# Gated delta rule inside a 256-token block: query scale as a logarithm in the gates, output norm from one product with ones, the value part of u from four whole products

## The chip, the cores and the metric

The kernel runs on one core of a Trainium2 chip. The metric is device time in microseconds (us) of one execution; lower is better. PE is TensorE (matmuls), PEld its weight loads, DVE is VectorE, ACT is ScalarE, POOL is GpSimd, SP issues DMAs.

## The reference, cut to what matters

The program computes a whole block: a mixer with a gated delta rule and cross attention, a second mixer, and a mixture of experts. Only the delta rule is touched. It has 24 value heads of width 128 over 256 tokens, in chunks of 64, with 12 query/key heads, each shared by two value heads:

```python
q = jnp.repeat(l2_norm(q), rep, axis=2) * DN_HEAD_DIM ** -0.5
k = jnp.repeat(l2_norm(k), rep, axis=2)
gc = jnp.cumsum(g, axis=-1)
...
sol = lax.linalg.triangular_solve(m, rhs, left_side=True, lower=True, unit_diagonal=True)
u0, w = sol[..., :dv], sol[..., dv:]
qk = jnp.einsum("bhncd,bhnjd->bhncj", q, k) * decay
q_dec = q * jnp.exp(gc)[..., None]
def step(state, inp):
    u = u0_c - jnp.einsum("bhcd,bhde->bhce", w_c, state)
    o = jnp.einsum("bhcd,bhde->bhce", qd_c, state) + jnp.einsum("bhcj,bhje->bhce", qk_c, u)
    state = cd_c[..., None, None] * state + jnp.einsum("bhcd,bhce->bhde", kd_c, u)
    return state, o
...
o = rms_norm(o.astype(p.dtype), out_g)
```

## The kernel before

All work is float32. Weights stream from memory in 466 units. Each unit has two halves. For each half ACT copies the weights to a rounded part (WH, line 2369, a CAST) and DVE makes the remainder (WL, line 1661), both three halves ahead of the matmuls that use them. PE then runs 24 matmuls of a half, in four pieces of six instructions. I call such a piece a fill. After a unit of the mixer's projections, ACT and DVE take the result out: for a value column by a convolution (ACT tap, three DVE operations, ACT Silu), for a gate column z by one ACT Silu.

The order on every engine is written by one class, `Plan`, that all engines replay. Each engine then executes its own list in order and waits on semaphores. In `mix`, two groups of two value heads are live at a time (a group is one query/key head; 12 groups), and after every step of a group one fill is put in. `group` (line 301) gives the steps of a group g:

- `dn_in`: PE makes X (inverse factors), A (k times q) and transposes of k and v into PSUM banks bA, bB, bC. It waits for `yn` of group g-2, which had the same buffers.
- `dn_decay`: DVE forms dT, the gap of summed gates (d1); ACT takes Exp of it (eT) and of qd (eB).
- `dn_uc`, `dn_low`, `dn_w`: PE products UC and W; ACT takes them out (un, nw); DVE scales k and v (k, v0), and multiplies A into dT (mark `qk`, line 1895), on POOL qd is multiplied by the query.
- four chunk steps: `dn_u(n)` on PE gives u in bank bA, ACT takes it out with the key's scale RNK (ut0 to ut3), `dn_o(n)` on PE gives the output o and the state's increment s, DVE adds it to the state (S0, S1, S2).
- `dn_y`: ACT takes the output out, POOL squares it. `dn_yss`: PE sums the squares over the head's width by four products into one column each; DVE adds the epsilon (scaled by the query's norm, EPSQ); ACT Sqrt; DVE reciprocal of 128x4. `dn_ybc`: PE spreads the 128x4 result over the partitions by four products. `dn_yn`: DVE multiplies it into the output.

Group g+2 starts when g ends, and the two live groups run about half a group apart. In steady state, while an odd group p ends (`dn_yss`, `dn_ybc`, `dn_yn`), the next even group e goes through `dn_decay`, `dn_uc`, `dn_low`, `dn_w` to its `dn_u(0)`. A pair below is the time from one even group's `dn_u(0)` to the next one's. Earlier, `rn_root` computes the scales of the 12 keys and queries, `iv_turn` transposes the summed gates, and `invert` inverts the chunk matrices on DVE.

Of the kernel before, what the change touches and what calls it, by code (L numbers as in the profile page):

```python
# [38 lines left out]
VEC = {}  # L39
# [126 lines left out]
class Plan:  # L166
# [485 lines left out]
def build(nc, D, out, scratch):  # L652
    ctx = ExitStack()
    with ctx:
# [30 lines left out]
        def f(kb, n):  # L685
            return view(kb, n, F)
# [110 lines left out]

        def dn_u(g):
            return dn(g, "US")[:, 0:256]

        def dn_s(g):
# [3 lines left out]
        IV_KK, IV_E, IV_TMP, IV_STG = f(94, 4096), f(110, 3072), f(78, 512), f(88, 1536)  # L805
        IV_GC, IV_BE, IV_GB = f(77, 64)[0:NI, :], f(77.25, 64)[0:NI, :], f(76, 256)[0:48, :]
        IV_U, IV_T = f(94, 2048), f(102, 2048)
        BEN = f(77.5, 48)
        EPSQ = vec[:, VEC["alog"][0]:VEC["alog"][0] + 24]
        iv_kk = IV_KK[0:NI, :].rearrange("p (r c) -> p r c", c=64)  # L810
# [228 lines left out]
        def tensor_program(e):  # L1039
# [340 lines left out]

            def dn_u_(g, n):
                bA = dn_bank(g)[0]
                t, b = n // 2, 64 * (n % 2)
                if n:
                    need_a(g, f"ut{n - 1}")
                    need_v(g, f"S{n - 1}")
                else:
                    need_a(g, "nw")
                    need_v(g, "qk")
                for h in range(2):  # L1390
                    i = 2 * h + t
                    o = PS[b:b + 64, bA, h * 128:h * 128 + 128]
                    m = mm(o, blk(dn(g, "U"), i)[:, b:b + 64], blk(dn(g, "bv"), i), True, n == 0)
                    if n:
                        m = mm(o, blk(dn(g, "X"), i)[:, b:b + 64], blk(dn_s(g), h), False, True)
                mark(g, f"u{n}", m)

            def dn_o(g, n):

                _, bB, bC = dn_bank(g)  # L1400
                t, b = n // 2, 64 * (n % 2)
                need_a(g, f"ut{n}")
                need_g(g, "qd")
# [5 lines left out]
                def from_within(h, start, stop):  # L1409
                    o = PS[:, bC, h * 256 + t * 128:h * 256 + t * 128 + 128]  # L1410
                    return mm(o, dn_u(g)[:, h * 128:h * 128 + 128], blk(dn(g, "dT"), 2 * h + t), start, stop)

# [9 lines left out]
                if n < 3:  # L1422
                    for h in range(2):
                        i = 2 * h + t
                        m = mm(blk(PS[:, bB, :], h), blk(dn(g, "kdc"), i)[b:b + 64, :],
                               dn_u(g)[b:b + 64, h * 128:h * 128 + 128], True, True)
                    mark(g, f"s{n}", m)

            def dn_yss(g):
                bA = dn_bank(g)[0]  # L1430
                need_g(g, "ysq")
                for i in range(4):
                    m = add_up(bA, i, blk(dn(g, "kb"), i))
                mark(g, "yss", m)

            def dn_ybc(g):
                bB = dn_bank(g)[1]
                need_v(g, "yrc")
                for i in range(4):
                    m = spread(blk(PS[:, bB, :], i), dn_s(g)[:, i:i + 1], C("ident"))  # L1440
                mark(g, "ybc", m)

# [189 lines left out]
            def end():  # L1632
                for d in range(4):
# [6 lines left out]
                  "iv_product": iv_product, "dn_in": dn_in, "dn_uc": dn_uc, "dn_w": dn_w, "dn_u": dn_u_, "dn_o": dn_o,  # L1640
                  "dn_yss": dn_yss, "dn_ybc": dn_ybc, "bias": bias, "ki_out": ki_out, "index": index,
                  "v2_turn": v2_turn, "aw": aw, "at": at_, "av": av, "pm": pm, "mean": mean, "stat": stat_,
# [4 lines left out]
        def vector_program(e):  # L1647
# [243 lines left out]
            def dn_low(g):  # L1891
# [20 lines left out]

            def dn_yss(g):
                rr = dn_s(g)[:, 0:4]
                eps = EPSQ[:, 2 * g:2 * g + 2].unsqueeze(1).broadcast_to([128, 2, 2])
                need_p(g, "yss")
                mark(g, "ysc", stt(rr.rearrange("p (h t) -> p h t", h=2),
                                   PS[:, dn_bank(g)[0], 0:4].rearrange("p (h t) -> p h t", h=2), 1.0 / 128, eps, ALU.mult,
                                   ALU.add))
                need_a(g, "yrt")  # L1920
                mark(g, "yrc", recip(rr, rr))

            def dn_yn(g):
                y = tile(VT, 2 * g, 2)
                need_p(g, "ybc")
                mark(g, "yn", stt(y, y, vc("outg"), PS[:, dn_bank(g)[1], :], ALU.mult, ALU.mult))

# [374 lines left out]
            def end():  # L2302
# [23 lines left out]
                for t in range(2):  # L2326
# [11 lines left out]
                  "rn_root": rn_root, "iv_product": iv_product, "iv_decay": iv_decay, "iv_scale": iv_scale,  # L2338
                  "iv_step": iv_step, "iv_out": iv_out, "dn_decay": dn_decay, "dn_uc": dn_uc, "dn_low": dn_low, "dn_o": dn_o, "dn_yss": dn_yss, "dn_yn": dn_yn, "y_split": y_split, "x1_out": x1_out,
                  "bias": bias, "ki_out": ki_out, "index": index, "topk": topk, "v2_turn": v2_turn, "aw": aw, "an": an,  # L2340
# [8 lines left out]
        def scalar_program(e):  # L2349
# [176 lines left out]
            def dn_u_(g, n):  # L2526
                t, b = n // 2, 64 * (n % 2)
                need_p(g, f"u{n}")
                mark(g, f"ut{n}", act(dn_u(g)[b:b + 64, :], PS[b:b + 64, dn_bank(g)[0], 0:256], ACT.Copy,
                                      scale=RNK[b:b + 64, 2 * g + t:2 * g + t + 1]))  # L2530

# [210 lines left out]
        def gpsimd_program(e):  # L2742
# [305 lines left out]
```

## Time and profile before

| | us |
|---|---|
| median of 3 runs | 2946.03 (2945.89 to 2946.81) |
| profiled execution, its own time | 2935.69 |
| its span from first to last instruction | 2933.9 |
| PE busy in the span | 2807.8 (96%) |
| DVE, ACT, POOL busy | 1926.1, 1371.3, 380.8 |

The profiled execution took 10.3 us less than the median of the timed runs. A busy engine is one with an instruction in it; instructions on PE overlap, so that a row's busy time divided by its count is closer to what one costs than its mean length. A plain float32 matmul stands as two instructions in the trace (x8 is four products).

### The profile page before, as it was taken

How to read it: one execution, taken by the hardware profiler on the slowest of the kernel's cores; microseconds unless marked ns; L12 is line 12 of the kernel's file. 1: busy time of each engine (PE TensorE's matmuls, PEld its weight loads, DVE VectorE, ACT ScalarE, POOL GpSimd, SP SyncE). 2: the span in 40 equal slices, each digit the busy share in tenths (PEclk: the TensorE clock that was granted, in tenths of full speed). 3: DMA queues.
4: the chain of work that ended last, by engine and by line, in shares of the span. 5: the costliest groups of instructions: out<-in, count | busy, mean ns of one | idle time of the engine just before them, and what ended most of it. 6: DMA issues, size and time to landing. Idle time of an engine off the chain costs nothing.

```text
span 2933.9 us, 46174 instructions
## 1 busy us (share of the span) xinstructions
PE 2807.8 (96%) x19298; PEld 2646.5 (90%) x19298; DVE 1926.1 (66%) x2862; ACT 1371.3 (47%) x2241; POOL 380.8 (13%) x360
## 2 busy tenths in 40 slices
PE   6999989999999999999989999998999999999996
PEld 6999989889989998999979999997888899987785
DVE  5546668544445445665458666776888888878886
ACT  5446544455545334444354114443555555555554
POOL 0000020211111000005000002221212111112210
PEclk9999999999999999999989999999999999999998
DMA  5444555523324554544425469998999988899993
GB/s 190 173 158 144 172 143 173 167 88 115 100 99 170 187 184 149 187 144 166 158 105 183 163 210 364 367 362 325 363 378 370 352 324 323 321 352 350 342 348 143
DMA packets 109679, 668.46 MB, mean 228 GB/s; under 512 B 25776, under 2 KB 26312, under 8 KB 31552
## 3 DMA queue, kind: packets, MB, share of 16 engines
q1 hardware_dynamic: 83808, 496.08, 46.6%
q0 software_dynamic: 24512, 164.97, 15.3%
q10 hardware_dynamic: 1152, 4.47, 0.4%
q8 instruction: 153, 2.51, 0.3%
q14 instruction: 54, 0.44, 0.0%
HBM read 651.54 MB, written 13.30 MB: 227 GB/s over the span
## 4 chain that ended last, share of the span: by engine, by line
PE 75%; DVE 12%; DMA 6%; ACT 5%; issue 2%; SPq 0%; POOL 0%; DVEq 0%; ACTq 0%
PE PS L1043 75%; DVE WL L1661 4%; DVE m L1652 3%; DMA raw<-in_pv 2%; ACT WH L2369 2%; DMA m<-in_pv,keep 2%; ACT m L2354 1%; DMA m<-s_kk 1%; DVE m L1861 1%; PE PS L1046 1%; DMA raw<-in_w_kv 1%; ACT m L2355 1%; DVE m L1858 0%; ACT L2354 0%; DMA raw<-in_pu 0%
## 5 line engine op out<-in xcount | busy, mean ns | idle before, releaser
L1661 DVE TENSOR_TENSOR WL<-raw,WH 128x1024 fp32r<-128x1024 f32 x804 | 986.7, 1236 | 643.4 <-ACT WH L2369 641.8
L2369 ACT CAST WH<-raw 128x1024 fp32r<-128x1024 f32 x804 | 837.7, 1046 | 516.2 <-PE PS L1043 381.3
L1043 PE MATMUL PS<-m_4096r,WH 128*128 128x256 f32 x5184 | 984.0, 290 | 24.8 <-DVE m_4096r L1652 10.3
L1043 PEld LDWEIGHTS PS<-m_4096r,WH 128*128 128x128 f32 x5184 | 815.6, 193 | 46.8 <-issue 13.9
L1043 PE MATMUL PS<-m_4096r,WL 128*128 128x256 f32 x2592 | 737.3, 284 | 0.0
L1043 PE MATMUL PS<-m_8192r,WH 128*128 128x256 f32 (+1 forms) x2560 | 558.9, 312 | 17.4 <-issue 11.1
L1043 PE MATMUL PS<-WH,m_896r 128*128 128x512 f32 x1536 | 522.8, 393 | 17.4 <-DVE m_896r L2287 17.4
L1043 PEld LDWEIGHTS PS<-m_4096r,WL 128*128 128x128 f32 x2592 | 500.6, 193 | 0.0
L1043 PEld LDWEIGHTS PS<-m_8192r,WH 128*128 128x128 f32 x2560 | 396.7, 193 | 20.4 <-issue 11.7
L1043 PE MATMUL PS<-m_8192r,WL 128*128 128x192 f32 (+1 forms) x1792 | 403.7, 272 | 0.0
L1043 PE MATMUL PS<-WL,m_896r 128*128 128x512 f32 x1024 | 401.3, 392 | 0.0
L1043 PEld LDWEIGHTS PS<-WH,m_896r 128*128 128x128 f32 x1536 | 290.8, 189 | 84.3 <-issue 11.9
L1043 PE MATMUL PS<-m,raw 128*128 128x192 f32 x2048 | 341.6, 326 | 0.0
L1043 PEld LDWEIGHTS PS<-m_8192r,WL 128*128 128x128 f32 x1792 | 333.9, 190 | 0.0
L1043 PEld LDWEIGHTS PS<-m,raw 128*128 128x128 f32 x2048 | 331.6, 190 | 0.1
L1043 PE MATMUL PS<-m 128*128 128x128 f32 (+4 forms) x1648 | 239.3, 285 | 21.7 <-ACT m L2629 7.4
L1043 PEld LDWEIGHTS PS<-m 128*128 128x128 f32 (+2 forms) x1648 | 205.4, 181 | 39.0 <-ACT m L2629 10.7
L1043 PEld LDWEIGHTS PS<-WL,m_896r 128*128 128x128 f32 x1024 | 194.1, 190 | 40.1
L2933 POOL DMA_INDIRECT m<-in_pv,keep x64 | 115.8, 1810 | 496.9 <-DVE m L1652 479.2
L1652 DVE SCALAR_TENSOR_TENSOR m<-m,keep 128x2048 f32<-128x2048 f32 (+1 forms) x67 | 152.9, 2283 | 7.1 <-DMA m<-in_pv,keep 7.0
L2194 DVE SCALAR_TENSOR_TENSOR m<-m 128x2048 f32<-128x2048 f32 x64 | 146.3, 2286 | 8.1 <-DMA m<-in_pun,keep 7.9
L2354 ACT ACTIVATE m<-m 128x256 f32<-128x256 f32 (+7 forms) x122 | 59.0, 500 | 154.2 <-DVE m L1652 117.9
(237 smaller groups left out, 1828.2 us busy)
## 6 DMA issues: line engine op xcount, KB each, us to landing
raw<-in_pu SPq DMA_DIRECT2D x128, 1024.0 KB, 6.8
raw<-in_pv SPq DMA_DIRECT2D x128, 1024.0 KB, 7.6
raw<-in_w_qkv SPq DMA_DIRECT2D x48, 1024.0 KB, 4.8
raw<-in_w_o SPq DMA_DIRECT2D x48, 1024.0 KB, 4.8
raw<-in_w SPq DMA_DIRECT2D x40, 1024.0 KB, 4.8
raw<-in_w_z SPq DMA_DIRECT2D x32, 1024.0 KB, 4.9
raw<-in_w_kv SPq DMA_DIRECT2D x16, 1024.0 KB, 4.9
raw<-in_w_q SPq DMA_DIRECT2D x16, 1024.0 KB, 4.8
```

What stands on the lines that cost most here:

```text
L1043: return e.matmul(o, l, x, start=start, stop=stop)
L1046: return e.transpose(o, i, C("ident"))
L1652: return e.scalar_tensor_tensor(out=o, in0=a, scalar=s, in1=b, op0=op0, op1=op1)
L1661: tt(WL[:, k, :], raw[:, n % NRAW, h * 1024:h * 1024 + 1024], WH[:, k, :].bitcast(F), ALU.subtract).then_inc(S["lo"], 1)
L1861: t = tt(iv_u[:, :, c, r], iv_u[:, :, c, r], tmp, ALU.subtract)
L2194: x = e.scalar_tensor_tensor(out=g, in0=g, scalar=1.0, in1=XS, op0=ALU.mult, op1=ALU.mult, accum_out=DOT[:, r:r + 1])
L2354: return e.activation(o, i, fn, scale=scale, bias=bias)
L2355: return e.activation(o, i, fn, scale=scale, bias=bias, accum_out=acc)
L2369: e.copy(WH[:, k, :], raw[:, n % NRAW, h * 1024:h * 1024 + 1024]).then_inc(S["hi"], 1)
L2933: e.indirect_dma_start(out=GB[b], out_offset=None, in_=D["pun" if k < 64 else "pv"], in_offset=bass.IndirectOffsetOnAxis(ap=EI[:, r:r + 1] ...
```

## The change

It has three parts.

1. The query's norm. Before, the query was used unnormed, and the epsilon of the output norm was scaled to make up for it. Now ACT takes a logarithm (Ln) of the query's sum of squares, DVE turns it into the logarithm of the query's scale (LNQ) and adds it to the summed gates (GCQ); a third transpose, a wider copy and a third slab in the scratch tensor `gb` take it to `qd`, from which dT and qd are made.
2. u. `dn_u(0)` now makes the value part of all four chunks by four whole 128x128 products (mark `ub`), and ACT takes it out by two operations of 128x256 into `bv`. `dn_u(1)` to `dn_u(3)` have two products instead of four, and DVE adds them to `bv` (ut1 to ut3, SCALAR_TENSOR_TENSOR of 64x256 that reads PSUM). ACT no longer works in these three.
3. The output norm. `dn_yss` is one product with a 128x128 matrix of ones, moving 512 columns, so that the sum stands in every partition; ACT takes Sqrt of 128x512 with the plain epsilon; a new DVE step `dn_yrc` takes two reciprocals of 128x256 where `dn_ybc` stood; `dn_ybc` and the 128x4 operations are gone.

```diff
-DN_PE = ("X", "A", "C", "UC", "W", "u0", "s0", "u1", "o1", "s1", "u2", "o2", "s2", "u3", "o3", "yss", "ybc")
-DN_V = ("d1", "k", "v0", "qk", "S0", "S1", "S2", "ysc", "yrc", "yn")
-DN_A = ("x", "eT", "eB", "un", "nw", "ut0", "ut1", "ut2", "ut3", "y", "yrt")
+DN_PE = ("X", "A", "C", "UC", "W", "ub", "s0", "u1", "o1", "s1", "u2", "o2", "s2", "u3", "o3", "yss")
+DN_V = ("d1", "k", "v0", "qk", "S0", "ut1", "S1", "ut2", "S2", "ut3", "yrc", "yn")
+DN_A = ("x", "eT", "eB", "un", "nw", "ub", "y", "yrt")
...
         self.do("dn_yss", g)
         for _ in range(WAITS[3]):
             yield
-        self.do("dn_ybc", g)
+        self.do("dn_yrc", g)
         yield
         self.do("dn_yn", g)
...
# PE, iv_turn
-                tr(PS[0:48, 2, 128:256], BEN).then_inc(S["iv_turn"], 1)
+                tr(PS[0:48, 2, 128:256], BEN)
+                tr(PS[0:48, 2, 256:384], GCQ).then_inc(S["iv_turn"], 1)
...
# PE, dn_u_
+                if n == 0:
+                    need_a(g, "un")
                     need_v(g, "qk")
+                    for i in range(4):
+                        m = mm(blk(PS[:, bA, :], i), blk(dn(g, "U"), i), blk(dn(g, "bv"), i), True, True)
+                    mark(g, "ub", m)
+                    return
+                need_a(g, "nw")
+                need_a(g, "ub")
+                need_v(g, f"S{n - 1}")
                 for h in range(2):
                     i = 2 * h + t
-                    o = PS[b:b + 64, bA, h * 128:h * 128 + 128]
-                    m = mm(o, blk(dn(g, "U"), i)[:, b:b + 64], blk(dn(g, "bv"), i), True, n == 0)
-                    if n:
-                        m = mm(o, blk(dn(g, "X"), i)[:, b:b + 64], blk(dn_s(g), h), False, True)
+                    m = mm(blk(PS[b:b + 64, bA, :], i), blk(dn(g, "X"), i)[:, b:b + 64], blk(dn_s(g), h), True, True)
...
# PE, dn_yss and dn_ybc
-                for i in range(4):
-                    m = add_up(bA, i, blk(dn(g, "kb"), i))
-                mark(g, "yss", m)
+                mark(g, "yss", mm(PS[:, dn_bank(g)[0], :], C("ones"), dn(g, "kb"), True, True))
-            def dn_ybc(g):
-                for i in range(4):
-                    m = spread(blk(PS[:, bB, :], i), dn_s(g)[:, i:i + 1], C("ident"))
...
# DVE, rn_root
-                ts(EPSQ, PS[:, 2, 0:24], 1e-6, 128e-6, ALU.add, ALU.mult)
+                v.step(ts(LNQ, LNQ, -0.5, -0.5 * math.log(128.0), ALU.mult, ALU.add))
+                v.own()
+                v.step(tt(by_head(GCQ), by_head(GC), per_group(LNQ), ALU.add))
...
# DVE, new
+            def dn_u_(g, n):
+                if n == 0:
+                    return
+                t, rows = n // 2, slice(64 * (n % 2), 64 * (n % 2) + 64)
+                need_p(g, f"u{n}")
+                need_a(g, "ub")
+                u = c4(dn(g, "bv"))[rows, t::2, :]
+                mark(g, f"ut{n}", stt(u, c4(PS[:, dn_bank(g)[0], :])[rows, t::2, :],
+                                      RNK[rows, 2 * g + t:2 * g + t + 1], u, ALU.mult, ALU.add))
+            def dn_yrc(g):
+                r = dn(g, "kdc")
                 need_a(g, "yrt")
+                for h in range(2):
+                    t = recip(tile(r, h), tile(r, h))
+                mark(g, "yrc", t)
...
# ACT, rn_root and dn_u_ and dn_yss
+                act(LNQ, PS[:, 2, 0:24], ACT.Ln, bias=C("eps6"))
                 act(RNK, PS[:, 2, 24:48], ACT.Sqrt, bias=C("eps6")).then_inc(S["rn_root"], 1)
+                for t in range(2):
+                    x = act(c4(dn(g, "bv"))[:, t::2, :], c4(PS[:, dn_bank(g)[0], :])[:, t::2, :], ACT.Copy,
+                            scale=RNK[:, 2 * g + t:2 * g + t + 1])
+                mark(g, "ub", x)
+                mark(g, "yrt", act(dn(g, "kdc"), PS[:, dn_bank(g)[0], :], ACT.Sqrt, scale=1.0 / 128, bias=C("eps6")))
```

The first place is DVE at the handover of an odd group to the next even one (group 5 ends, group 6 is before its `dn_u(0)`). m_512 are a group's buffers, dn_a and dn_v the semaphores of ACT and DVE (0 for even, 1 for odd groups), hi that of the CASTs. Before:

```order
L1888 TENSOR_TENSOR m_512<-PS,keep 128x256 x2
L1661 TENSOR_TENSOR WL<-raw,WH 128x1024 [waits hi]
L1895 TENSOR_TENSOR m_512<-m_512,PS 128x512 [waits dn_a0]
L1652 SCALAR_TENSOR_TENSOR m_6144<-m_6144,vecs,PS 128x512 [waits dn_pe1]
L1661 TENSOR_TENSOR WL<-raw,WH 128x1024 [waits hi]
```

After:

```order
L1884 TENSOR_TENSOR m_512<-PS,keep 128x256 x2
L1655 TENSOR_TENSOR WL<-raw,WH 128x1024 [waits hi]
L1923 RECIPROCAL m_512<-m_512 128x256 [waits dn_a1]
L1923 RECIPROCAL m_512<-m_512 128x256
L1891 TENSOR_TENSOR m_512<-m_512,PS 128x512 [waits dn_a0]
L1646 SCALAR_TENSOR_TENSOR m_6144<-m_6144,vecs,m_512 128x512 [waits dn_v1]
L1655 TENSOR_TENSOR WL<-raw,WH 128x1024 [waits hi]
```

The two reciprocals of group 5 stand behind a WL and ahead of group 6's `qk` (L1895 before, L1891 now). The second place is DVE a little later, from the first state of group 6 to `dn_uc` of group 7. Before:

```order
L1907 COPY m_512<-PS 128x128
L1652 SCALAR_TENSOR_TENSOR m_512<-m_512,keep,cons 128x128 [waits dn_v1,ld_u1]
L1652 SCALAR_TENSOR_TENSOR m_512<-m_512,keep,cons 128x128 x3
L1661 TENSOR_TENSOR WL<-raw,WH 128x1024 [waits hi]
L1884 TENSOR_TENSOR m_512<-PS,keep 128x512 [waits dn_pe1]
```

After:

```order
L1913 COPY m_512<-PS 128x128
L1646 SCALAR_TENSOR_TENSOR m_512<-m_512,keep,cons 128x128 [waits dn_v1,ld_u1]
L1646 SCALAR_TENSOR_TENSOR m_512<-m_512,keep,cons 128x128 x3
L1655 TENSOR_TENSOR WL<-raw,WH 128x1024 [waits hi]
L1646 SCALAR_TENSOR_TENSOR m_512<-PS,keep,m_512 64x2x128 [waits dn_a0,dn_pe0]
L1880 TENSOR_TENSOR m_512<-PS,keep 128x512 [waits dn_pe1]
```

The update ut1 of the even group, which was on ACT, now stands on DVE behind a WL. The place of every fill and step on PE is as before.

## Rows read from the trace of the kernel before

**Rows 1.** The page: each engine's busy time, share of the span and instructions.

```profile
PE 2807.8 (96%) x19298; PEld 2646.5 (90%) x19298; DVE 1926.1 (66%) x2862; ACT 1371.3 (47%) x2241; POOL 380.8 (13%) x360
```

**Rows 2.** Stretches: length, busy of PE, PEld, DVE, ACT, POOL, then PEclk, DMA share, GB/s.

```profile
548.00:913.00 365.00, 351.68 (x2749) 326.78 (x2747) 158.99 (x295) 189.70 (x281) 56.17 (x55) 0.99 0.31 99
...
735.40:795.40 60.00, 59.23 (x469) 55.10 (x469) 25.19 (x48) 32.43 (x48) 9.46 (x9) 1.00 0.35 106
```

**Rows 3.** Timeline 728.9 to 737, PE, ACT and DVE: start, length, instruction.

```profile
730.09 0.55 ACT L2519 ACTIVATE m<-PS 32x128 f32<-32x128 f32 x2 [1.16 <-PE PS L1043]
...
730.61 1.05 PE L1043 MATMUL PS<-cons,m 128*128 128x128 f32 x8
...
731.42 0.48 PE L1043 MATMUL PS<-m_4096r,WH 128*128 128x256 f32 x2
...
732.23 1.04 ACT L2369 CAST WH<-raw 128x1024 fp32r<-128x1024 f32 x1
...
733.30 1.22 DVE L1661 TENSOR_TENSOR WL<-raw,WH 128x1024 fp32r<-128x1024 f32 x1 [3.70 <-ACT WH L2369]
...
733.65 1.05 PE L1043 MATMUL PS<-m 128*128 128x128 f32 x8
...
734.45 0.68 DVE L1895 TENSOR_TENSOR m<-m,PS 128x512 f32<-128x512 f32 x1
734.47 0.48 PE L1043 MATMUL PS<-m_4096r,WH 128*128 128x256 f32 x2
...
735.40 0.65 PE L1043 MATMUL PS<-m 128*64 128x128 f32 x4
735.98 0.50 PE L1043 MATMUL PS<-m_4096r,WH 128*128 128x256 f32 x2
```

**Rows 4.** Timeline 749.5 to 750.6, PE: `dn_u(2)` of group 6 and the next fill.

```profile
749.52 1.09 PE L1043 MATMUL PS<-m 128*64 128x128 f32 x8
750.54 0.39 PE L1043 MATMUL PS<-m_4096r,WH 128*128 128x256 f32 x1
```

**Rows 5.** Groups of the whole span by form: busy, mean ns | idle before.

```profile
L1043 PE MATMUL PS<-m,cons 128*64 128x512 f32 x8 | 3.6, 598 | 0.0
...
L1676 DVE RECIPROCAL m<-m 128x256 f32<-128x256 f32 x2 | 3.5, 1752 | 3.5 <-ACT m L2354 3.5
```

**Rows 6.** Groups of 548 to 913 by form: a DVE operation from PSUM of 254 columns.

```profile
L1652 DVE SCALAR_TENSOR_TENSOR m<-PS,vecs,m 128x254 f32<-128x254 f32 x9 | 4.3, 482 | 0.3
```

**Rows 7.** Timeline 745.7 to 746.3: ut1 of group 6, WL, `dn_o(1)` of group 6.

```profile
745.71 0.47 ACT L2354 ACTIVATE m<-PS,keep 64x256 f32<-64x256 f32 x1
745.72 1.23 DVE L1661 TENSOR_TENSOR WL<-raw,WH 128x1024 fp32r<-128x1024 f32 x1 [3.85 <-ACT WH L2369]
...
746.23 1.74 PE L1043 MATMUL PS<-m 128*128 128x128 f32 x12 [0.77 <-ACT m L2354]
```

**Rows 8.** Timeline 714 to 724.2: `dn_u(3)` of group 5, WL, `yn` of group 4.

```profile
714.60 1.09 PE L1043 MATMUL PS<-m 128*64 128x128 f32 x8 [0.97 <-DVE m L1652]
...
717.30 1.23 DVE L1661 TENSOR_TENSOR WL<-raw,WH 128x1024 fp32r<-128x1024 f32 x1 [2.75 <-ACT WH L2369]
...
723.06 0.74 DVE L1652 SCALAR_TENSOR_TENSOR m<-m,vecs,PS 128x512 f32<-128x512 f32 x1
```

**Rows 9.** Timeline 379 to 384.3: `rn_root` on ACT and DVE, `iv_turn` on PE.

```profile
379.96 1.28 ACT L2354 ACT_TABLE_LOAD   x1
...
382.11 0.28 ACT L2354 ACTIVATE keep<-PS,cons 128x24 f32<-128x24 f32 x1 [0.87 <-PE PS L1043]
...
383.10 0.21 DVE L1800 TENSOR_TENSOR keep<-keep 128x48 f32<-128x48 f32 x1
...
384.12 0.27 PE L1046 MATMUL PS<-cons,keep 128*48 128x128 f32 x1
```

**Rows 10.** A wait of PE (timeline), and the stretch just behind it (columns as in rows 2).

```profile
559.99 1.74 PE L1043 MATMUL PS<-m 128*128 128x128 f32 x12 [1.44 <-ACT m L2354]
...
561.84:565.25 3.41, 3.41 (x16) 3.19 (x17) 2.74 (x7) 1.04 (x1) 0.00 (x0) 0.50 0.75 293
```

More of the change, by code:

```diff
@@ L796, in dn @@
             return f(108 + 2 * ((k - 3) % 10) if g % 2 else 88 + 2 * k, 512)
-        def dn_u(g):
-            return dn(g, "US")[:, 0:256]
         def dn_s(g):
@@ L805, in build @@
         IV_KK, IV_E, IV_TMP, IV_STG = f(94, 4096), f(110, 3072), f(78, 512), f(88, 1536)
-        IV_GC, IV_BE, IV_GB = f(77, 64)[0:NI, :], f(77.25, 64)[0:NI, :], f(76, 256)[0:48, :]
+        IV_GC, IV_BE, IV_GB = f(77, 64)[0:NI, :], f(77.25, 64)[0:NI, :], f(75, 384)[0:48, :]
         IV_U, IV_T = f(94, 2048), f(102, 2048)
         BEN = f(77.5, 48)
-        EPSQ = vec[:, VEC["alog"][0]:VEC["alog"][0] + 24]
+        LNQ = vec[:, VEC["alog"][0]:VEC["alog"][0] + 24]
+        GCQ = f(77.75, 48)
         iv_kk = IV_KK[0:NI, :].rearrange("p (r c) -> p r c", c=64)
@@ L826, in gc_rows @@
         def gc_rows(g):
-            return bass.AP(scratch["gb"].tensor, scratch["gb"].offset + 512 * g, [[0, 128], [1, 512]])
+            return bass.AP(scratch["gb"].tensor, scratch["gb"].offset + 12288 + 512 * g, [[0, 128], [1, 512]])
         def t_sem(g):
@@ L1401, in dn_o @@
                 t, b = n // 2, 64 * (n % 2)
-                need_a(g, f"ut{n}")
+                if n:
+                    need_v(g, f"ut{n}")
+                else:
+                    need_a(g, "ub")
                 need_g(g, "qd")
@@ L1410, in from_within @@
                     o = PS[:, bC, h * 256 + t * 128:h * 256 + t * 128 + 128]
-                    return mm(o, dn_u(g)[:, h * 128:h * 128 + 128], blk(dn(g, "dT"), 2 * h + t), start, stop)
+                    return mm(o, blk(dn(g, "bv"), 2 * h + t), blk(dn(g, "dT"), 2 * h + t), start, stop)
                 for h in range(2):
@@ L1425, in dn_o @@
                         m = mm(blk(PS[:, bB, :], h), blk(dn(g, "kdc"), i)[b:b + 64, :],
-                               dn_u(g)[b:b + 64, h * 128:h * 128 + 128], True, True)
+                               blk(dn(g, "bv"), i)[b:b + 64, :], True, True)
                     mark(g, f"s{n}", m)
             def dn_yss(g):
-                bA = dn_bank(g)[0]
                 need_g(g, "ysq")
-                for i in range(4):
-                    m = add_up(bA, i, blk(dn(g, "kb"), i))
-                mark(g, "yss", m)
-            def dn_ybc(g):
-                bB = dn_bank(g)[1]
-                need_v(g, "yrc")
-                for i in range(4):
-                    m = spread(blk(PS[:, bB, :], i), dn_s(g)[:, i:i + 1], C("ident"))
-                mark(g, "ybc", m)
+                mark(g, "yss", mm(PS[:, dn_bank(g)[0], :], C("ones"), dn(g, "kb"), True, True))
             def bias():
@@ L1640, in tensor_program @@
                   "iv_product": iv_product, "dn_in": dn_in, "dn_uc": dn_uc, "dn_w": dn_w, "dn_u": dn_u_, "dn_o": dn_o,
-                  "dn_yss": dn_yss, "dn_ybc": dn_ybc, "bias": bias, "ki_out": ki_out, "index": index,
+                  "dn_yss": dn_yss, "bias": bias, "ki_out": ki_out, "index": index,
                   "v2_turn": v2_turn, "aw": aw, "at": at_, "av": av, "pm": pm, "mean": mean, "stat": stat_,
@@ L1911, in dn_o @@
                 mark(g, f"S{n}", t)
[L1913 to L1919, printed above, removed]
+            def dn_yrc(g):
+                r = dn(g, "kdc")
                 need_a(g, "yrt")
-                mark(g, "yrc", recip(rr, rr))
+                for h in range(2):
+                    t = recip(tile(r, h), tile(r, h))
+                mark(g, "yrc", t)
             def dn_yn(g):
                 y = tile(VT, 2 * g, 2)
-                need_p(g, "ybc")
-                mark(g, "yn", stt(y, y, vc("outg"), PS[:, dn_bank(g)[1], :], ALU.mult, ALU.mult))
+                need_v(g, "yrc")
+                mark(g, "yn", stt(y, y, vc("outg"), dn(g, "kdc"), ALU.mult, ALU.mult))
             def y_split(c):
@@ L2338, in vector_program @@
                   "rn_root": rn_root, "iv_product": iv_product, "iv_decay": iv_decay, "iv_scale": iv_scale,
-                  "iv_step": iv_step, "iv_out": iv_out, "dn_decay": dn_decay, "dn_uc": dn_uc, "dn_low": dn_low, "dn_o": dn_o, "dn_yss": dn_yss, "dn_yn": dn_yn, "y_split": y_split, "x1_out": x1_out,
+                  "iv_step": iv_step, "iv_out": iv_out, "dn_decay": dn_decay, "dn_uc": dn_uc, "dn_low": dn_low, "dn_u": dn_u_, "dn_o": dn_o, "dn_yrc": dn_yrc, "dn_yn": dn_yn, "y_split": y_split, "x1_out": x1_out,
                   "bias": bias, "ki_out": ki_out, "index": index, "topk": topk, "v2_turn": v2_turn, "aw": aw, "an": an,
@@ L2496, in iv_turn @@
                 crossed(a)
-                e.copy(IV_GB, PS[0:48, 2, 0:256]).then_inc(S["iv_gates"], 1)
+                e.copy(IV_GB, PS[0:48, 2, 0:384]).then_inc(S["iv_gates"], 1)
             def iv_exp(b):
@@ L2526, in dn_u_ @@
             def dn_u_(g, n):
[L2527 to L2530, printed above, removed]
+                if n:
+                    return
+                need_p(g, "ub")
+                for t in range(2):
+                    x = act(c4(dn(g, "bv"))[:, t::2, :], c4(PS[:, dn_bank(g)[0], :])[:, t::2, :], ACT.Copy,
+                            scale=RNK[:, 2 * g + t:2 * g + t + 1])
+                mark(g, "ub", x)
             def dn_y(g):
@@ L2536, in dn_yss @@
             def dn_yss(g):
-                need_v(g, "ysc")
-                mark(g, "yrt", act(dn_s(g)[:, 0:4], dn_s(g)[:, 0:4], ACT.Sqrt))
+                need_p(g, "yss")
+                mark(g, "yrt", act(dn(g, "kdc"), PS[:, dn_bank(g)[0], :], ACT.Sqrt, scale=1.0 / 128, bias=C("eps6")))
             def y_split(c):
@@ L3038 @@
                "h": nc.dram_tensor("s_h", (128, 2, 2048), F, kind="Internal").ap(),
-               "gb": nc.dram_tensor("s_gb", (2, 24, 2, 128), F, kind="Internal").ap(),
+               "gb": nc.dram_tensor("s_gb", (3, 24, 2, 128), F, kind="Internal").ap(),
                "kk": nc.dram_tensor("s_kk", (24, 2, 64, 64), F, kind="Internal").ap(),
```

8 lines of the change are left out of this document (2 added, 6 removed).

## The prediction

> **What bounds the kernel now.** I read the page first. PE is busy for 96% of the span [rows 1], so the first guess for any change is the PE work that it takes away. Then I cut out the delta rule with the view of stretches: in 548 to 913 us PE is busy 351.7 of 365 us, DVE 159 and ACT 190 [rows 2]. A steady pair of groups takes 60.0 us, and PE idles in less than 1 us of it [rows 2]. So the average says that PE bounds and that DVE, at 42%, has room. The average hides something, for which I read the timeline. DVE idles mostly in front of WL operations, while it waits for the CAST of ACT [rows 3, 7, 8]. Everything behind a WL in DVE's list waits with it, although DVE counts as idle. At three places of the pair PE already starts a step just when such a chain has ended: `dn_u(0)` of the even group at 735.40, 0.27 us after `qk` ended at 734.45 + 0.68 [rows 3]; `dn_o(1)` of the even group, which waited 0.77 us for ut1 [rows 7]; `dn_u(3)` of the odd group, which waited 0.97 us for DVE [rows 8]. The order rows above show that the change puts DVE work into two of these chains.
>
> **PE work taken away.** Prices are distances between starts. `dn_u(n)` with eight instructions takes 750.54 - 749.52 = 1.02 us [rows 4], with four 735.98 - 735.40 = 0.58 [rows 3]: 0.44 saved in each of three steps. `ub` has eight of the kind of `dn_w`, 734.47 - 733.65 = 0.82, instead of 0.58: 0.24 more. `dn_ybc` took 731.42 - 730.61 = 0.81 [rows 3], all of it saved. The new `dn_yss` is two instructions of 512 columns at 3.6/8 = 0.45 each [rows 5], 0.9 us; it replaces eight that cost about what those of `dn_ybc` do, 0.8. I take no difference. Sum for a group: 3 x 0.44 - 0.24 + 0.81 = 1.89 us, for 12 groups 22.7 us, if PE alone bounds. The rest asks which of it survives.
>
> **The odd group's reciprocals.** One of 128x256 takes 1.752 us [rows 5]; two take 3.5, or 3.4 with their overlap of about 0.1. Before, the chain from `un` (730.09) over a table load, Silu and CAST to the end of WL at 734.52 and to the end of `qk` at 735.13 [rows 3] met PE at `dn_u(0)`. It hangs on UC, not on `dn_ybc`, so the 0.81 us that PE saves there do not shorten it. The reciprocals stand between WL and `qk`, and `ub` needs `qk`. So `ub` starts 3.4 us later after UC than `dn_u(0)` did, and PE waits 3.4 + 0.81 = 4.2 us there. This happens at the five handovers.
>
> **ut1 on DVE.** ut1 of the even group took 0.47 us on ACT right after the CAST, beside WL [rows 7]. Now it comes behind that WL, which ends at 746.95, and takes about 0.48 us, by a DVE operation from PSUM of nearly its width of 482 ns [rows 6]. `dn_o(1)` then starts at 747.45 instead of 746.23, 1.2 us later, and 0.24 more since the chain starts from the longer `ub`: 1.45. The bounds: were it as short as ACT's end of it, 0.8; with one more WL ahead, 2.7. Behind ut1 on DVE are queued `dn_uc` of the odd group and S1; PE reaches them with some 1.5 us to spare. The other ut come behind no late WL in my walk, but for ut3 of the even group (some 0.1 us).
>
> **The rest of the pair.** After `dn_o(1)` the steps run at PE's pace. I follow how late each is against before: +1.45 at `dn_o(1)` of the even group; -0.44 (u2), +0.24 (`ub` of the odd group), -0.44 (u3), -0.44 and -0.44 (u1, u2 of the odd group) gives -0.07 at the wait for S2. That wait of 0.97 us [rows 8] shrinks by some 0.7, as ysc and the small reciprocal no longer stand ahead of S2; then u3 gives -0.44 and `dn_ybc` -0.81: about -2.05. The even group's own reciprocals start behind the WL of 717.30 [rows 8], which moves 1.2 to 2.4 us earlier with PE and with the ut that ACT no longer takes out, and end between 719.6 and 720.8. The next WL (before at 721.92) and `yn` (723.06, 0.74 long) [rows 8] follow at PE's new pace plus what the CAST gives, and `dn_in` of the next group waits about 0.2 for it. So UC of the next group is 1.9 us earlier than before, and `ub` 3.4 - 1.9 = 1.5 us later: **a pair gets 1.5 us longer**, not 3.8 shorter.
>
> **The sum of the chains.** Four such pairs: +6.0. The first pair has value columns, whose convolution and Silu stand between the even group's reciprocals and its `yn`, so that it gains almost nothing (0.3) before the odd wait: +3.1. The last pair has no successor: it gains 1.9 + 0.81 and small change, -3.0. In `rn_root` ACT loads a table early, under other work, and the Sqrt runs at 382.11; DVE is done at 383.31 and PE comes at 384.12 [rows 9], a slack of 0.8. Now Ln takes that place (0.28) and a second load of 1.28 us [rows 9] stands behind it, and DVE gets two small operations (0.3): 1.86 - 0.8 = +1.05. Bounds for it are 0 and 1.9. The built program has one table load more, this one. The wider copy and the third slab of `gb` ride under `invert`, whose load lands before it is used; uncovered they would cost some tenths. Sum: 6.0 + 3.1 - 3.0 + 1.05 = +7.2 us.
>
> The Trainium skill, page "ScalarE: Activation LUTs", section "What ACT_TABLE_LOAD costs", says that every switch costs the load and a drain, 2.66 us together. By it the term of `rn_root` would be 2.4 us and the sum 8.6. The load's own row of 1.28 agrees; of a drain the timeline shows nothing, since the next ACT operation starts some 0.03 us behind a load. I go by the row.
>
> **The clock.** In the timeline PE waited 1.44 us ahead of 559.99, and from 561.84 to 565.25 the granted clock was 0.50, which is 1.2 instead of 2.4 GHz [rows 10]. Over the 3.41 us PE does half its work, up to 1.7 us lost. Shorter waits like that of rows 7 were not followed by a fall. The change makes five waits of 4.2 us ahead of `ub` and six of about 2.4 ahead of `dn_o(1)` (0.77 + 1.2 + 0.44). If each of the first kind and half of the second bring one such stretch of about 1.5 us, that is 12 us, less the two that the stage has now: +9. The bounds are 0, and 11 x 1.7 = 19. I take +7, as some lost time lies ahead of the next wait and hides in it.
>
> **Total.** +7.2 + 7 = +14 us: the profiled execution 2935.7 becomes 2950. The median of the runs stood 10.3 above it, so the forecast is 2960.
>
> **The rivals.**
>
> *PE's savings come through (faster).* The 96% speaks for it. If `qk` is ready in time all the same, because the WL ahead of the reciprocals comes some 4 us earlier than in rows 3, the five waits and most of the clock term vanish, and the pair gains 1.9 us and more: 5 x -1.9 - 3 + 1 = -11, up to the -22.7 of pure PE work: 2923 to 2935. It decides once the delay of `qk` is under 1.9 us. Against it speaks that this WL depends on UC itself. 0.15. The Trainium skill, page "Perfetto Trace Analysis", section "Identifying the Most-Contended Engine", would have one optimize the engine with the highest occupancy first; by that rule the change comes out on this side. The rows above on chains inside one pair disagree.
>
> *The terms cancel (same).* The clock hardly falls, and the waits are a little shorter (reciprocals overlap a late WL): between -5 and +6, 2941 to 2952. 0.19.
>
> *DVE falls behind for good (much slower).* If the even group's reciprocals delay `yn` and `dn_in` as well by some 2 us, as they may in pairs with convolutions, and ut3 waits behind WL each time, the pair gets 4 us longer: 6 x 4 + 10 of clock = +34, 2980. 0.09.
>
> *The forecast's own case* is +6 to +26: 0.57.
>
> **Numbers.** A measurement of this kernel can tell about 0.2%, 5.9 us. Faster 0.17 (the first rival and a little of the second), same 0.18, slower 0.65. The range leaves out the far ends of the first and third rivals: 2934 to 2976. The forecast's own case alone is 2952 to 2972.
>
> **What would show it.** Right: PE waits of about 4 us ahead of the 128x128 products in bA, ended by DVE's `qk`, five times; in DVE's timeline WL, two RECIPROCAL of 1.75, `qk`; `dn_o(1)` waits over 2 us for a SCALAR_TENSOR_TENSOR; pairs of 61 to 64 us; stretches of granted clock 0.50 behind the long waits; PE's busy time in the stage down by some 20 us at equal clock. Wrong: pairs of 57 us or less with `qk` early, or long waits without a fall of the clock. What would break the walk is a reciprocal that takes another time in this place, or a WL that comes earlier than I derive.

## The result and the profile after

The changed kernel takes 2983.43 us (median of 4 runs, 2979.08 to 2987.98), the kernel before, in runs beside it, 2945.96 us (2945.76 to 2946.81). The ratio is 1.0127, with a 95% interval of 1.0111 to 1.0143: slower, by 37.5 us. The prediction had forecast +14 us (2960); its direction is right, its size is not, and the time is outside the range (2934 to 2976). The profiled execution is the longest of the four, 2987.98 us, with a span of 2986.2.

The page of the changed kernel, busy time by engine, against [rows 1]:

```profile
PE 2820.8 (94%) x19035; PEld 2651.1 (89%) x19035; DVE 1982.4 (66%) x2899; ACT 1364.2 (46%) x2219; POOL 388.0 (13%) x360
```

PE has 263 instructions less and is busy 13 us *longer*. Fewer instructions in more busy time suggests that some of them ran slower, and the view of stretches shows where. From here on "the stage" is the delta rule, cut between the same two WL operations in every kernel (the 149th and the 213th of the program), since they mark the same work. Before (length, busy of PE, PEld, DVE, ACT, POOL, then PEclk, DMA share, GB/s):

```profile
532.50:910.40 377.90, 364.07 (x2852) 338.97 (x2852) 169.00 (x314) 196.94 (x292) 59.69 (x60) 0.99 0.32 104
```

After, the same stage; then one pair, from the beginning of one wait ahead of `ub` to the beginning of the next; two stretches at half clock in that pair; and the undisturbed end of it:

```profile
532.00:951.10 419.10, 370.67 (x2590) 339.17 (x2589) 224.17 (x350) 190.00 (x268) 59.22 (x58) 0.91 0.30 93
...
752.76:819.69 66.93, 60.31 (x416) 55.03 (x416) 33.72 (x53) 30.32 (x43) 8.88 (x8) 0.90 0.30 92
755.59:762.42 6.83, 5.80 (x27) 5.80 (x28) 2.77 (x4) 1.52 (x4) 2.27 (x2) 0.50 0.19 78
772.66:779.49 6.83, 6.83 (x30) 5.94 (x29) 3.93 (x8) 1.04 (x1) 0.00 (x0) 0.50 0.34 138
785.00:815.00 30.00, 29.76 (x225) 26.68 (x222) 18.20 (x27) 16.23 (x20) 4.96 (x5) 1.00 0.36 99
```

The stage is 419.1 - 377.9 = 41.2 us longer. PE's idle time in it went from 13.8 to 48.4 us (length less busy), and its mean granted clock from 0.99 to 0.91. A pair takes 66.9 us, where the one of [rows 2] took 60.0. In a stretch at 0.50, which is 1.2 GHz, PE is busy nearly all the time and gets 27 to 30 instructions done in 6.83 us; at 1.00 it does 225 in 30 us, 51 in 6.83. In the record of the granted clock I count 13 such stretches in the stage, nine of 6.83 us and four of 3.41, together 75.1 us; before there were two, together 6.8. The mean of 0.91 agrees: 0.09 of 419.1 us, times two, is 75 us.

The waits of PE in the stage, by the releaser's line (us in total, times, longest). L1891 is `qk`, and L1646 is the helper of DVE's SCALAR_TENSOR_TENSOR, so ut, S and `yn`:

```profile
PE PS L1041 <- DVE m L1646: 24.8, 13, 3.4
...
PE PS L1041 <- DVE m L1891: 21.9, 5, 4.8
```

The timeline of the changed kernel around the handover at 752 us, DVE and PE, answers to [rows 3] and [rows 7] (start, length, instruction, idle time before it and its releaser):

```profile
751.52 1.23 DVE L1655 TENSOR_TENSOR WL<-raw,WH 128x1024 fp32r<-128x1024 f32 x1 [3.65 <-ACT WH L2372]
752.66 3.36 DVE L1923 RECIPROCAL m<-m 128x256 f32<-128x256 f32 x2
755.94 0.63 DVE L1891 TENSOR_TENSOR m<-m,PS 128x512 f32<-128x512 f32 x1
756.62 1.22 PE L1041 MATMUL PS<-m 128*128 128x128 f32 x4 [3.87 <-DVE m L1891]
...
769.98 1.23 DVE L1655 TENSOR_TENSOR WL<-raw,WH 128x1024 fp32r<-128x1024 f32 x1 [3.85 <-ACT WH L2372]
771.24 0.49 DVE L1646 SCALAR_TENSOR_TENSOR m<-PS,keep,m 64x256 f32<-64x256 f32 x1
771.79 0.82 PE L1041 MATMUL PS<-m 128*128 128x128 f32 x5 [2.52 <-DVE m L1646]
```

Both chains are there as the prediction drew them: WL, two reciprocals, `qk`, `ub`; and WL, ut1, `dn_o(1)`. DVE sat idle for 3.65 and 3.85 us ahead of each WL, with the work that PE needed queued behind it.

In `rn_root` (timeline, against [rows 9]) the second table load and the wait of PE:

```profile
381.81 0.28 ACT L2357 ACTIVATE vecs<-PS,cons 128x24 f32<-128x24 f32 x1 [0.86 <-PE PS L1041]
382.10 1.28 ACT L2357 ACT_TABLE_LOAD   x1
383.40 0.28 ACT L2357 ACTIVATE keep<-PS,cons 128x24 f32<-128x24 f32 x1
...
384.88 0.29 PE L1044 MATMUL PS<-cons,keep 128*48 128x128 f32 x1 [0.90 <-DVE keep L1796]
```

Outside the stage the profiled execution has 11.1 us more (2567.1 against 2556.0). All of it lies behind the stage, where the two kernels do the same work: the stage begins at 532.0 and 532.5 us. The profiles of the experiments spread from 2559.6 to 2573.8 us outside it, so I don't put these 11 us down to the change. (The four kernels with the old u stand at 2556.0 to 2561.4 there, the six with the new one at 2562.7 to 2573.8; whether that is chance, one profile of each can't tell.)

### The profile page after: what moved, and what is told of

Its sections match the earlier page's. It is cut to its first block, busy times and chain, and to the rows that moved or that the text cites. A ratio compares the mean times of both kernels' runs of the same rounds, so it can differ in the third digit from the quotient of the medians.

```text
span 2986.2 us, 45663 instructions
## 1 busy us (share of the span) xinstructions
PE 2820.8 (94%) x19035; PEld 2651.1 (89%) x19035; DVE 1982.4 (66%) x2899; ACT 1364.2 (46%) x2219; POOL 388.0 (13%) x360
## 4 chain that ended last, share of the span: by engine, by line
PE 71%; DVE 13%; DMA 8%; ACT 6%; issue 2%; POOL 0%; SPq 0%; DVEq 0%; ACTq 0%
PE PS L1041 70%; DMA raw<-in_pv 5%; DVE WL L1655 5%; DVE m L1646 4%; ACT WH L2372 3%; DMA m<-in_pv,keep 1%; ACT m L2357 1%; DVE m L1923 1%; ACT L2357 1%; PE PS L1044 1%; DMA raw<-in_w_kv 1%; ACT m L2358 0%; DMA m<-s_kk 0%; DVE m L1857 0%; DVE m L2197 0%
## 5 line engine op out<-in xcount | busy, mean ns | idle before, releaser
L1041 PE MATMUL PS<-m_4096r,WH 128*128 128x256 f32 x5184 | 995.3, 293 | 23.8 <-DVE m_4096r L1646 9.8
L1041 PEld LDWEIGHTS PS<-m_4096r,WH 128*128 128x128 f32 x5184 | 824.7, 195 | 50.8 <-issue 17.3
L1041 PE MATMUL PS<-m_8192r,WH 128*128 128x256 f32 (+1 forms) x2560 | 563.0, 314 | 16.1 <-issue 11.1
L1041 PE MATMUL PS<-m 128*128 128x128 f32 (+4 forms) x1552 | 247.6, 301 | 56.3 <-DVE m L1646 24.8
L1041 PEld LDWEIGHTS PS<-m 128*128 128x128 f32 (+2 forms) x1552 | 212.3, 200 | 75.1 <-DVE m L1646 29.0
L1646 DVE SCALAR_TENSOR_TENSOR m<-m,keep 128x2048 f32<-128x2048 f32 (+1 forms) x67 | 152.9, 2283 | 6.3 <-DMA m<-in_pv,keep 6.2
L2940 POOL DMA_INDIRECT m<-in_pun,keep x64 | 85.9, 1342 | 326.4 <-DVE m L2197 318.4
```

The costliest lines, as they stand in the source:

```text
L1041: return e.matmul(o, l, x, start=start, stop=stop)
L1646: return e.scalar_tensor_tensor(out=o, in0=a, scalar=s, in1=b, op0=op0, op1=op1)
L2940: e.indirect_dma_start(out=GB[b], out_offset=None, in_=D["pun" if k < 64 else "pv"], in_offset=bass.IndirectOffsetOnAxis(ap=EI[:, r:r + 1] ...
```

## The experiments

Two theories stand against the one of the prediction (A: two chains on DVE make PE wait, and each wait is paid again by half clock). B: it is the amount of DVE work in the stage, 169.0 us before and 224.2 now, wherever it stands. C: the clock falls by itself, and the waits are not its cause.

**e1_norm_before.** The third part is undone, so that only the chain of ut1 is left (the cut shows the part on PE; DVE and ACT go back in the same way):

```diff
-        self.do("dn_yrc", g)
+        self.do("dn_ybc", g)
...
-                mark(g, "yss", mm(PS[:, dn_bank(g)[0], :], C("ones"), dn(g, "kb"), True, True))
+                bA = dn_bank(g)[0]
+                for i in range(4):
+                    m = add_up(bA, i, blk(dn(g, "kb"), i))
```

> The changed kernel with its third part undone: norm by 128x4 sums, small reciprocal and the spreading products; the new u and the gates stay. Theory A (two chains through DVE, each wait followed by a stretch of half clock): the 4.7 us waits ahead of ub vanish, the waits of some 2.5 us ahead of the even group's dn_o(1) stay, with their half-clock stretches of up to 6.8 us; 2950 to 2962. Theory B (DVE simply has more work, the place does not matter): the share of DVE work taken off is two thirds, so two thirds of the 37 us go: 2958, but spread over many small waits, and no long wait anywhere. Theory C (the clock falls by itself, whatever the waits): as many half-clock stretches as in the changed kernel, above 2970.

Measured: 2968.76 us (2958.63 to 2970.01, 4 runs), ratio 1.0076 [1.0050, 1.0102]. Its waits in the delta rule, and the stage:

```profile
PE PS L1041 <- DVE m L1655: 25.2, 15, 3.4
```

```profile
534.20:926.90 392.70, 364.23 (x2755) 339.94 (x2754) 187.56 (x350) 184.48 (x268) 60.91 (x60) 0.95 0.31 100
```

The long waits ahead of `ub` are gone (the largest left there is 0.7). Those ahead of the even groups' `dn_o(1)` are as in the changed kernel (3.18, 3.18, 2.50, 2.50, 2.51 and 3.42 us). The clock fell to half seven times, for 37.5 us: once at each of these six waits, and once at another of 2.27 us. So such waits come with a fall of the clock without a 4 us wait ahead of them. The time is above my 2962, and long waits are there, where B had expected none. Only 14.8 of its 25 us lie in the stage by this profile; where the rest is stays open.

**e2_u_before.** The second part is undone (u as before), so that only the reciprocals' chain is left:

```diff
-                if n == 0:
-                    need_a(g, "un")
+                if n:
+                    need_a(g, f"ut{n - 1}")
+                    need_v(g, f"S{n - 1}")
+                else:
+                    need_a(g, "nw")
                     need_v(g, "qk")
...
+                    m = mm(o, blk(dn(g, "U"), i)[:, b:b + 64], blk(dn(g, "bv"), i), True, n == 0)
```

> The changed kernel with its second part undone: u by 14 half products, taken out by ACT; the new norm and the gates stay. Theory A: the waits ahead of dn_u(0) of the even groups stay at about 4.2 to 4.7 us and each is followed by half clock; the waits ahead of dn_o(1) go back below 1.5 us; chains give about +12, clock about +15: 2968 to 2978. Theory B: DVE keeps its reciprocals, two thirds of the loss: 2970. Theory C: above 2975.

Measured: 2974.28 us (2963.04 to 2982.49, 4 runs), ratio 1.0113 [1.0089, 1.0138]. The waits of PE in the stage (L1889 is `qk`, L2345 the ut on ACT):

```profile
PE PS L1044 <- DVE m L1889: 22.3, 5, 4.9
PE PS L1044 <- ACT m L2345: 6.0, 6, 1.4
```

Waits of 3.96 to 4.90 us stand at the five handovers, each with a fall of the clock that began in it or within 0.5 us behind it. `dn_o(1)` waits 0.77 us as in [rows 7], and 1.44 us in the two pairs with value columns. The stage is 400.0 us long. Each part by itself makes the kernel slower, by 25.2 and 30.7 us of the medians; together they cost 37.5, less than the sum (each part was timed beside runs of the kernel before, 2943.61 us there and 2945.96 for the whole).

**e3_recip_behind_qk.** The whole change, but the odd group's reciprocals behind `qk`, in front of their `yn`:

```diff
-            def dn_yrc(g):
+            def dn_yrc(g, last=False):
+                if g % 2 and g < 11 and not last:
+                    return
...
             def dn_yn(g):
                 y = tile(VT, 2 * g, 2)
+                if g % 2 and g < 11:
+                    dn_yrc(g, True)
```

> The changed kernel with one move in DVE's list: the two reciprocals of an odd group stand behind the next even group's qk, just ahead of yn. No work is added or removed. Theory A: ub starts about 3.4 us earlier, a new wait of about 2.8 us stands ahead of dn_in of the next odd group, which needs yn; 1.4 us less a pair and perhaps fewer half-clock stretches: 2965 to 2978. Theory B: the same work on DVE, no difference: 2983. Theory C: no difference either.

Measured: 2972.43 us (2964.76 to 2988.13, 4 runs), ratio 1.0116 [1.0083, 1.0148]. The waits:

```profile
PE PS L1041 <- DVE m L1646: 35.8, 18, 3.4
PE PS L1041 <- DVE m L1891: 5.8, 5, 1.6
```

Ahead of `ub` 5.8 us are left of 21.9, but five waits of 2.19 us for `yn` came up, ahead of the next odd group's `dn_in`. The wait moved one step on. In the profiled execution the stage is 400.2 us, 18.9 shorter than in the changed kernel with the same DVE work (224.6 us), and half clock in it 37.5 instead of 75.1 us; by B it should not be shorter at all. In the times the gain is not resolved: the medians are 11 us apart, but the two ratios' intervals overlap.

**e4_filled_waits.** The whole change, and in the waits PE does useless products into a bank that is free then: 8 of 256 columns ahead of `ub`, 5 ahead of the even group's `dn_o(1)`. DVE's chains are untouched; only PE is not idle while it waits for them.

```diff
+            def keep_warm(g, k):
+                for _ in range(k):
+                    mm(PS[:, dn_bank(g)[2], 0:256], C("ident"), C("eye")[:, 0:256], True, True)
...
+                    if g % 2 == 0 and g:
+                        need_v(g, "v0")
+                        keep_warm(g, 8)
                     need_v(g, "qk")
...
+                    if n == 1 and g % 2 == 0:
+                        keep_warm(g, 5)
                     need_v(g, f"ut{n}")
```

> The changed kernel with useless products of constants on PE in the two waits (8 of 256 columns, about 3.4 us, ahead of ub of an even group; 5, about 2.1 us, ahead of its dn_o(1)), into a bank that nobody reads then; the result is unchanged. Theory A: the chains stay as long, but PE is busy through them, so the half-clock stretches behind them vanish; their cost is about half of the 75 us at half clock in the delta rule's stage, less the 7 us of before, some of it hidden: 2950 to 2963. Theory C: the clock falls all the same, 2983 or more. If the waits alone, not the clock, are the loss, then 2980 to 2985.

Measured: 2961.71 us (2961.21 to 2963.19, 4 runs), ratio 1.0063 [1.0045, 1.0081]. The stage, and 20 us that hold both waits of a pair, where the changed kernel has two stretches at half clock:

```profile
531.70:928.10 396.40, 378.13 (x2733) 342.75 (x2733) 223.66 (x350) 190.22 (x268) 60.27 (x59) 0.97 0.30 98
745.00:765.00 20.00, 19.23 (x132) 16.97 (x131) 12.21 (x21) 8.68 (x14) 3.54 (x3) 1.00 0.31 108
```

The same two places in its timeline, with the useless products (two instructions each) and the short rest of the wait:

```profile
745.13 3.62 PE L1041 MATMUL PS<-cons 128*128 128x256 f32 x16
749.16 0.49 PE L1041 MATMUL PS<-m 128*128 128x128 f32 x2 [0.41 <-DVE m L1900]
...
758.93 2.32 PE L1041 MATMUL PS<-cons 128*128 128x256 f32 x10
761.60 0.66 PE L1041 MATMUL PS<-m 128*128 128x128 f32 x4 [0.35 <-DVE m L1655]
```

Work that yields nothing makes the kernel 2983.43 - 2961.71 = 21.7 us faster by the medians (19 by the ratios to before, 1.0127 - 1.0063), and the stage 22.7 us shorter. Half clock in the stage fell from 75.1 to 20.5 us, and what is left of it lies ahead of 655 us, in the pairs with value columns: three stretches at waits of 2.3 us that are not filled, and one from 562.66 us, 2.2 us behind the 1.02 us that are left of a filled wait. Behind 655 us the stage has none, where the changed kernel had eight. C is refuted: in the filled waits of those pairs the clock stays at full. B has no place for this gain either: DVE's work is the same 224 us.

**e5_gates_only.** The first part alone (parts 2 and 3 as before); of its edit against the kernel before:

```diff
-                ts(EPSQ, PS[:, 2, 0:24], 1e-6, 128e-6, ALU.add, ALU.mult)
+                v.step(ts(LNQ, LNQ, -0.5, -0.5 * math.log(128.0), ALU.mult, ALU.add))
...
+                act(LNQ, PS[:, 2, 0:24], ACT.Ln, bias=C("eps6"))
```

> Only the first part of the change: the query's scale as a logarithm in the gates; u and the output norm as before (with the plain epsilon). Theory A: one wait of about 0.9 us ahead of iv_turn, nothing in the groups: +0 to +2, so 2943 to 2948. Theory B gives the same. If the first part costs more than the walk said (the wider copy, the third slab), 2950 or more.

Measured: 2941.15 us (2928.75 to 2953.36, 10 runs) beside 2941.92 of before (31 runs), ratio 1.0006 [0.9984, 1.0028]: no difference. The logarithm and its table load cost nothing that can be measured, so the loss lies in parts 2 and 3.

**e6_ut_ahead_of_wl.** The whole change, and DVE's WL of a half one place later in its list, in the units of the delta rule only: it stands one fill further back, and so behind the step of the delta rule that is put in there. No work is taken away.

```diff
+LATE = (73, 104)
...
+            def held(q):
+                return 2 * LATE[0] <= q < 2 * LATE[1]
+
             def prep(q):
+                if held(q):
+                    return
...
+            def unit_mm(n, h, part, per):
+                if held(2 * n + h) and part == 1:
+                    lo_part(2 * n + h + 3)
```

> The whole changed kernel, with DVE's WL of each half in the delta rule's units put one step later in DVE's list: ut1 then stands ahead of the WL, and the odd group's reciprocals ahead of the WL that waits for its CAST, so that they run while DVE used to idle. No work is added or removed. Theory A: both waits (4.7 and 2.5 us) fall below 1 us, the half-clock stretches behind them go, and the PE work taken away comes through: 2922 to 2940, faster than the kernel before. Theory B (DVE's amount of work): no difference to 2983. Theory C (the clock falls by itself): 2950 to 2970.

Measured: 2930.83 us (2924.60 to 2941.95, 10 runs), ratio 0.9964 [0.9943, 0.9984]: faster than the kernel before by some 11 us, and than the changed one by some 50. The stage, and one pair:

```profile
533.20:894.30 361.10, 338.90 (x2594) 312.01 (x2593) 224.01 (x350) 189.52 (x269) 64.04 (x60) 0.99 0.34 108
727.37:783.32 55.95, 53.93 (x417) 49.60 (x416) 33.37 (x53) 30.26 (x43) 9.75 (x8) 1.00 0.36 110
```

DVE's timeline at a handover, and PE behind it:

```profile
722.48 3.35 DVE L1933 RECIPROCAL m<-m 128x256 f32<-128x256 f32 x2
726.14 1.23 DVE L1656 TENSOR_TENSOR WL<-raw,WH 128x1024 fp32r<-128x1024 f32 x1 [0.31 <-ACT WH L2382]
727.29 0.68 DVE L1901 TENSOR_TENSOR m<-m,PS 128x512 f32<-128x512 f32 x1
...
728.02 0.71 PE L1042 MATMUL PS<-m 128*128 128x128 f32 x4 [0.65 <-DVE m L1901]
```

The reciprocals take as long as ever, but they now run in the 3.65 us in which DVE stood idle ahead of WL: its idle time there is 0.31 us. `ub` waits 0.65 us instead of 3.87. DVE's work in the stage is the same 224 us, which refutes B. PE's waits in the stage:

```profile
PE PS L1042 <- DVE m L1901: 10.0, 5, 4.0
PE PS L1042 <- DVE m L1647: 10.0, 8, 2.3
```

Two long ones are left, 3.98 and 3.15 us, in the pairs with convolutions; each has a stretch at half clock of 3.41 us, which began in the last 0.5 us of the wait, and the clock fell nowhere else in the stage. All in all PE idles 22.2 us in the stage, against 13.8 before, and is busy 25.2 us less: 16.8 us shorter.

**e7_norm_before_ut_ahead.** The same move of WL on e1:

```diff
-            def dn_yrc(g):
+            def dn_yss(g):
...
+            def unit_mm(n, h, part, per):
+                if held(2 * n + h) and part == 1:
+                    lo_part(2 * n + h + 3)
```

> The new u and the gates with the norm as before, and the same later place of WL. Theory A: the waits ahead of dn_o(1) go; PE saves 3 x 0.44 - 0.24 = 1.1 us a group: 2928 to 2942, some 5 to 10 us above the kernel that keeps the new norm, since the spreading products stay. Theory B: like the run with the norm as before, 2969. Theory C: 2955 or more.

Measured: 2934.39 us (2925.91 to 2942.64, 10 runs), ratio 0.9972 [0.9956, 0.9989]. No wait in its stage is over 2.3 us, and the clock is never at half there. It can't be told from e6: with the chains out of the way, the third part neither gains nor loses what could be measured. Its stage is 362.4 us against 361.1. PE is busy 345.3 us in it, against 338.9, and idle 17.1, against 22.2: what the third part saves of PE's work goes for the most part into waits.

**e8_before_late_wl.** The control: the same move of WL (the edit of e6) on the kernel before, with nothing of the change.

> The kernel before with nothing but the later place of WL. It tells how much of a gain is due to that place alone. Theory A: small, since only S2 and qk stood behind a WL: the 0.97 us wait for S2 may shrink, 2936 to 2946. Theory B: no difference.

Measured: 2946.80 us (2935.69 to 2951.68, 10 runs), ratio 1.0017 [0.9998, 1.0036]: no difference, and its stage is 377.8 us, against 377.9. The wait for S2, which I had expected to shrink, is 2.04 us instead of 0.97 in two pairs, and other waits are shorter. So the later WL is worth nothing by itself; in e6 it lets the change's own saving come through. Timed side by side, e6 is 16.0 us faster than this control, which agrees with the 16.7 us between their stages.

## Why the prediction was wrong

The measured median lies 23.4 us above the forecast. The chains were priced about right; the step that failed is the clock, taken at +7 us, where the runs show +31.8.

**PE work taken away: right.** The prediction had 22.7 us for the 12 groups. At equal clock (0.99 both) PE is busy 364.07 us in the stage before and 338.90 in e6: 25.2 less.

**The odd group's reciprocals: right.** Forecast: a wait of 4.2 us five times, released by `qk`. Measured: 4.67, 4.67, 3.87, 3.87 and 4.81. Two reciprocals took 3.36 us.

**ut1 on DVE: right.** Forecast: `dn_o(1)` waits about 2.4 us in six even groups. Measured: 2.50 to 2.52 three times, 3.17, 3.18 and 3.42 in the rest. Not foreseen: three more waits of 2.3 us for DVE in the pairs with value columns. Two of them are new, ahead of products that need another ut behind a late WL (from 576.37 and 652.41 us), of which the prediction's walk had none. The third is `dn_in` waiting for an even group's `yn`, which had waited 1.66 us there before. Undone one by one (e1, e2), each chain loses its own waits and keeps the other's.

**The sum of the chains: nearly right.** In the stage the change takes away 25.2 us of PE work and adds 48.4 - 13.8 = 34.6 us of waiting: +9.4. The prediction's chains there give 6.0 + 3.1 - 3.0 = +6.1. With the clock on top, a pair takes 66.9 us, where the prediction had 61 to 64.

**`rn_root`: right.** Forecast 1.05 us of new waiting, measured 0.90 in the changed kernel, and nothing in the time of e5. The drain that the Trainium skill, page "ScalarE: Activation LUTs", section "What ACT_TABLE_LOAD costs", adds to a load isn't seen: the ACTIVATE behind the load of 382.10 + 1.28 starts at 383.40, and the wait came out below my term, not at the 2.4 us of that rule. The load's own 1.28 us agree.

**The clock: this step failed.** Its mechanism was right and its size was not. The prediction took one stretch of 3.41 us behind each long wait and behind half of the others, 1.5 us lost in each, in all +7, and set the bound at 19. Measured, by the same PE work at two clocks: 370.67 us (2590 instructions) in the changed kernel against 338.90 us (2594) in e6, 31.8 us lost. So the stage's 41.2 us are -25.2 of PE work, +34.6 of waiting and +31.8 of clock. The record of the clock agrees: 75.1 - 6.8 = 68.3 us more at half speed, half of them 34.2, less what lies in waits. Two things were mis-sized. I had the length of a stretch from the stage's two, both of 3.41 us behind waits of less than 1.5 us [rows 10], while nine of the 13 here were twice as long, each a loss of some 6.83/2 = 3.4 us. And I counted only half of the waits of 2.4 us as followed by a fall, while all six were; of 14 waits over 2 us, 13 had a fall, each between 1.6 us ahead of the wait's end and 0.9 us behind it. The bound of 19 us rested on the length of those short stretches, so it was no bound. The trace of the kernel before had a closer case, outside the stage: a wait of PE of 3.53 us, and with it a stretch twice as long (timeline, then the stretch).

```profile
436.16 0.79 PE L1043 MATMUL PS<-m_4096r,WH 128*128 128x256 f32 x2 [3.53 <-DVE m L1652]
```

```profile
435.54:442.37 6.83, 6.21 (x29) 6.21 (x30) 5.17 (x12) 4.15 (x6) 2.21 (x4) 0.50 0.46 119
```

At 3.4 us for each of the 11 waits, the same sum would have had a bound of some 37 us, an estimate from this row. The experiment with filled waits gives the causal side: some 20 us come back when PE isn't idle in them. The clock's 31.8 - 7 = 24.8 us are about the whole of the miss.

**The rivals.** That the terms cancel fell with the clock. That DVE falls behind for good gave the nearest number (2980), which was luck in the main. Its mechanism was 2 us more for `yn` and `dn_in` and a late ut3 in each of six pairs. Of that, the trace of the changed kernel has one wait of `dn_in` for `yn`, 2.29 us instead of 1.66 (from 602.70 us), and the two late ut above, all in the pairs with value columns; the steady pairs have none, and DVE's work alone did no harm in e6. The first rival, PE's savings come through, named what decides it: the delay of `qk` under 1.9 us. In e6 PE waits only 0.65 us for `qk`, and the pair takes 55.95 us, where full saving would give 60.0 - 3.8 = 56.2. The rule of the Trainium skill's page "Perfetto Trace Analysis", section "Identifying the Most-Contended Engine", to optimize the engine of the highest occupancy first (for TensorE the page goes by the busy share of the weight loads, 90% in [rows 1], which is the highest too), is borne out by e6 and not by the change as it stands: the same PE work was taken away in both.

## What to carry to other kernels

An engine that is 42% busy has no room for an operation that someone waits for, if its list puts that operation behind one that waits for a slow producer: price new work by the place in the in-order list, and look first whether it fits into an idle gap ahead of such a wait. When a tensor engine that was nearly always busy gets waits of 2 to 5 us, count them twice, once as idle time and once as half clock; here the second cost (31.8 us) was about as large as the first (34.6). And a bound that rests on stretches behind short waits doesn't hold for long ones: look through the whole trace for a wait of the length that the change will make.

## What was not expected of the hardware

A wait of 2.50 us by itself (e1, from 755.98 us) was followed by a fall of the granted clock from 2.4 to 1.2 GHz, 2.2 us behind its end. The fall is not tied to a wait's length in a simple way: one of 1.44 us is followed by a fall in the kernel before [rows 10], one of the same length at the same step in e2 is not; 2.26 us from 652.41 in the changed kernel is not, and of two of 2.27 us in e1 the one from 578.87 is not and the one from 646.61 is. Stretches lasted 3.41 or 6.83 us in this stage. Useless products of TensorE in its waits paid for themselves (e4). What decides whether one wait brings a fall, and how long it lasts, stays open.
